# Two terms of a split product as one 512-column matmul in the feed-forward output and down projections

## The chip, the cores and the metric

The kernel runs on one core of a Trainium2 chip. The metric is device time in microseconds, the median of several executions. TensorE multiplies; its weight loads have a row of their own in the profile (PEld), because a load can lie under the matmul before it. VectorE (DVE), ScalarE (ACT) and GpSimd (POOL) do elementwise work, SyncE (SP) issues the transfers of the weights. PSUM, where matmuls write, is here one tensor `bank` of eight banks, each 512 fp32 wide on each of the 128 partitions.

## The reference, cut to what matters

The program is two layers of one transformer block and two layers of another on 256 tokens of width 1024. The places of this change are the second products of the feed-forward parts:

```
def _swiglu(x, w_in, w_out):
    gate, up = jnp.split(x @ w_in, 2, axis=-1)
    return (jax.nn.silu(gate) * up) @ w_out
...
h = h + 0.5 * g1[:, None, :] * _swiglu(hn, ffn1_w_in[l], ffn1_w_out[l])     # D_FF = 2816
...
h = h + 0.5 * g3[:, None, :] * _swiglu(hn, ffn2_w_in[l], ffn2_w_out[l])
...
return x + jnp.square(jax.nn.relu(h @ w_up)) @ w_down                       # 4 * 1024 wide inside
```

The output must be as exact as fp32 products.

## The kernel before

**Split products.** A matmul on fp32 data is slow, one on rounded data (fp32r) is fast but inexact. So each factor is held as two rounded parts, the high part and the rest, and a product is three terms: high weight times high input, high weight times low input, low weight times high input. `terms` (lines 714 to 720) issues them one after another into the same 256 columns of a PSUM bank. Each matmul loads its 128x128 block of weights first, so the high weights are loaded twice.

**Where the weights come from.** SyncE fills a ring of four slots (`ring`) by DMA, 256 columns of the weights at a time ("a chunk"). ScalarE rounds a half chunk into `w_hi` (line 1210), GpSimd subtracts it from the ring and leaves the rest in `w_lo` (line 685), and TensorE waits for that (`half_ready`). `w_hi` and `w_lo` hold two chunks, so there are four half chunks in flight, and ScalarE may overwrite a half when TensorE has used it.

**Order of the work.** All engines run hand-ordered lists. For each of the two layers of part one: `ffn("f1")`, the mixing stage (projection "z", attention, projection "o"), `ffn("f2")`. For each of the two layers of part two: the projection "z2" with attention between its pieces, "y" and "wo", "up" and "dn". An `ffn` is an input product of 22 chunks of 8 tiles (line 719 with `hn` and `hn_lo`), and the output product `out_product` with 4 groups of 256 output columns. In a group the inner 2816 are 22 tiles of 128, brought in four chunks of 6, 6, 5 and 5 tiles; in "dn" there are 32 tiles in four chunks of 8. A group has two output tiles `c` of 128 rows (the weight's columns) by 256 tokens; each has a bank of its own, of which the first 256 columns are used. In each half chunk `out_product` does all tiles of `c` = 0, then all of `c` = 1.

**Inputs of the product.** `gated` (feed-forward) and `up2` (down) hold for each tile the high part (index 0) and the low part (index 1), 256 columns each, side by side.

**After a group.** VectorE adds the bank to the residual `h`: line 1709 (`stt`: bank times gate plus `h`) in `ffn`, line 2070 (`tt`) after "dn", once for `c` = 0, once for `c` = 1. ScalarE squares the new `h` (line 1238), VectorE sums the squares (`add_squares`, line 1626), TensorE sums over the partitions (lines 815 and 818), ScalarE makes the root (lines 1244 and 1246), and the scaled `h` feeds the next stage's first product (lines 750, 751 and 754). That chain stands at the end of each `ffn` and each "dn"; nothing else can feed TensorE in it.

**Small fp32 products.** Some matmuls take unrounded fp32: the attention scores (line 934), group sums (line 1012, 512 columns), the projections "o" and "wo" (line 805), the sums of ada weights (line 842).

Of the kernel before, what the change touches and what calls it, by code (L numbers as in the profile page):

```python
# [20 lines left out]
ALU = mybir.AluOpType  # L21
# [5 lines left out]
S = 256  # L27
# [284 lines left out]
def out_bank(g, c):  # L312

    return 2 - 2 * (g % 2) + c
# [73 lines left out]
def build(nc, dram, out, at, old):  # L389

    plan = Plan()
    with ExitStack() as ctx:
# [307 lines left out]
        def _(pe):  # L700
# [60 lines left out]
                        last.then_inc(weights_used, eng.step(f"used {phase} {i}" if half else  # L761
                                                             f"half used {phase} {i}", weights_used))

            def out_product(phase, chunks, x, outs, done, free, last_x):

                total = sum(k_tiles(phase, i)[1] for i in chunks)
                for i in chunks:
                    q = split_slot(phase, i)  # L770
                    if last_x and i == chunks[-1]:
                        pe.wait_ge(parts_done, eng.at(last_x))
                    for half, (k0, n) in enumerate(halves(phase, i)):
                        half_ready(phase, i, half)
                        for c in range(2):
                            if i == chunks[0] and half == 0:
                                for by, mark in free[c:c + 1]:
                                    pe.wait_ge(by, eng.at(mark))
                            ws = slice(c * P, (c + 1) * P)
                            for k in range(n):  # L780
                                kx, kw = k_tiles(phase, i)[0] + k0 + k, half * 4 + k
                                last = terms(outs[c], w_hi[:, q, kw, ws], w_lo[:, q, kw, ws], x[:, kx, 0], x[:, kx, 1],
                                             False, kx == 0, kx == total - 1)
                            if c == 1:
                                last.then_inc(weights_used, eng.step(f"used {phase} {i}" if half else
                                                                     f"half used {phase} {i}", weights_used))
                            elif half and i == chunks[-1]:
                                last.then_inc(tensor_done, eng.step(done))
# [105 lines left out]
            def ffn(s, layer, following):  # L894
                for p in range(PAIRS):
                    for r in range(2):
                        b = bank[:, 2 * (p % 2) + r].rearrange("p (c s) -> p c s", c=2)
                        free = ((silu_done, f"{s} hi {p - 2}") if r else (parts_done, f"{s} gated {p - 2}"),)
                        product(s + "in", (2 * p + r,), (b[:, 0], b[:, 1]), first=s if p == r == 0 else None,
                                free=free if p >= 2 else ())  # L900
                    if (s, p) in (("f1", 9), ("f2", 8)):
                        ada_fold(layer, 0 if s == "f1" else 2)
                for g in range(4):
                    out_product(s + "out", tuple(range(4 * g, 4 * g + 4)), gated,
                                (bank[:, out_bank(g, 0), 0:S], bank[:, out_bank(g, 1), 0:S]), f"{s} out {g}",
                                ((vector_done, f"h {following} {2 * g - 4}"), (vector_done, f"h {following} {2 * g - 3}"))
                                if g >= 2 else ((parts_done, f"{s} gated {PAIRS - 2}"),) if g == 0 else (),
                                f"{s} gated {PAIRS - 1}" if g == 0 else None)
# [174 lines left out]
            for layer in eng.layers("two"):  # L1083
# [62 lines left out]
                        norm_sum("up")  # L1146
                for g in range(4):
                    out_product("dn", tuple(range(4 * g, 4 * g + 4)), up2,
                                (bank[:, 2 * (g % 2), 0:S], bank[:, 2 * (g % 2) + 1, 0:S]), f"dn out {g}",
                                ((vector_done, f"h {AFTER_DN[layer]} {2 * g - 4}"), (vector_done, f"h {AFTER_DN[layer]} {2 * g - 3}"))  # L1150
                                if g >= 2 else ((parts_done, "up split 13"),) if g == 0 else (),
                                "up split 15" if g == 0 else None)
# [418 lines left out]
        def _(dve):  # L1571
# [105 lines left out]
            def ffn(s, gate_at, layer, following):  # L1677
                for p in range(PAIRS):
                    j = p % 2
                    if (s, p) == ("f2", 9):  # L1680
                        modulation(layer, 64, 72, (layer, 17))
                    of = ada_chunk(s + "in", p, layer)
                    if of:
                        ada_sum(*of)
                    dve.wait_ge(silu_done, eng.at(f"{s} silu {p}"))
                    dve.wait_ge(weights_used, eng.at(f"used {s}in {2 * p + 1}"))
                    tt(bank[:, 2 * j], act_tmp[:, j], bank[:, 2 * j + 1], ALU.mult) \  # L1687
                        .then_inc(vector_done, eng.step(f"{s} mult {p}"))
                    dve.wait_ge(silu_done, eng.at(f"{s} hi {p}"))
                    tt(gated[:, 2 * p:2 * p + 2, 1, :], bank[:, 2 * j].rearrange("p (c s) -> p c s", c=2),  # L1690
                       gated[:, 2 * p:2 * p + 2, 0, :], ALU.subtract).then_inc(parts_done, eng.step(f"{s} gated {p}", parts_done))
                if s == "f1":
                    modulation(layer, 16, 48, (layer, 11))
                ts(der[:, 24:32], mod[:, gate_at:gate_at + 8], 0.5, None, ALU.mult) \
                    .then_inc(vector_done, eng.step())
                dve.wait_ge(vector_done, eng.at())
                for g in range(4):
                    of = ada_chunk(s + "out", g, layer)
                    if of:
                        ada_sum(*of)  # L1700
                    if g:
                        add_squares(following, g - 1)
                    for c in range(2):
                        k = 2 * g + c
                        if c == 0:
                            dve.wait_ge(tensor_done, eng.at(f"{s} out {g}"))
                        else:
                            dve.wait_ge(weights_used, eng.at(f"used {s}out {4 * g + 3}"))
                        stt(h[:, k], bank[:, out_bank(g, c), 0:S], col(der, 24 + k), h[:, k], ALU.mult, ALU.add) \
                            .then_inc(vector_done, eng.step(f"h {following} {k}"))  # L1710

            def maxima(hd, tile, maps=(0, 1, 2)):
                st = stat[:, hd.u % 4]
# [262 lines left out]
            for layer in eng.layers("two"):  # L1976
# [84 lines left out]
                for g in range(4):  # L2061
                    if g:
                        add_squares(AFTER_DN[layer], g - 1)
                    for c in range(2):
# [2 lines left out]
                            dve.wait_ge(tensor_done, eng.at(f"dn out {g}"))  # L2067
                        else:
                            dve.wait_ge(weights_used, eng.at(f"used dn {4 * g + 3}"))
                        tt(h[:, k], bank[:, 2 * (g % 2) + c, 0:S], h[:, k], ALU.add) \  # L2070
                            .then_inc(vector_done, eng.step(f"h {AFTER_DN[layer]} {k}"))
                        if layer + 1 == L:
                            dve.wait_ge(vector_done, eng.at())
                            ts(result[:, k], h[:, k], col(norm2, 32 + k), None, ALU.mult) \
# [24 lines left out]
```

## Time and profile before

| what | value |
|---|---|
| median of 3 executions | 2004.17 us (2003.87, 2004.17, 2008.47) |
| span of the profiled execution | 2008.3 us |
| execution nearest to it by time, with what lies around the span | 2008.47 us |
| TensorE busy | 1929.0 us, 96% of the span, 15200 matmuls and as many loads |
| GpSimd busy | 1321.1 us, 66% |
| ScalarE busy | 940.1 us, 47% |
| VectorE busy | 837.2 us, 42% |
| chain that ended last | TensorE 84%, line 719 alone 68% |

Busy time of TensorE says only that some matmul was in its pipeline: matmuls overlap, and a 256-column one is recorded with some 280 ns while the next begins less than 120 ns later. The distance from one start to the next is what costs time; it is read from starts in the timeline, or from a merged piece of the chain of waits divided by its count. Times in the rows are in microseconds from the start of the span, mean durations in ns.

### The profile page before, as it was taken

The page shows a single profiled execution, that of the slowest core. Times are in us where ns is not written, and L with a number is a line of the kernel's source. Part 1 is how long each engine was busy: PE and PEld are TensorE (multiplying, and loading weights), DVE is VectorE, ACT ScalarE, POOL GpSimd, SP SyncE. Part 2 cuts the span into 40 slices and gives each one's busy share as a digit, 9 for nine tenths or more (in the row PEclk, how much of TensorE's full clock was granted, in tenths as well). Part 3 has the DMA queues.
Part 4 walks back from the last instruction along what each step waited for, and adds up shares of the span by engine and source line. Part 5 has one row for each costly group of instructions (what it writes and reads, how often), then busy time and mean ns, then how long its engine had stood idle before and what let it go on. Part 6 is the DMA issues. An engine that isn't in the chain of part 4 may idle for free.

```text
span 2008.3 us, 36107 instructions
## 1 busy us (share of the span) xinstructions
PE 1929.0 (96%) x15200; PEld 1859.7 (93%) x15200; DVE 837.2 (42%) x1753; ACT 940.1 (47%) x1467; POOL 1321.1 (66%) x612
## 2 busy tenths in 40 slices
PE   6999997999999999889999999999999999999999
PEld 3999995899999998779999999989999999999999
DVE  3774676372148467735112532233311622233322
ACT  2544454344454445445444445525544445535543
POOL 0878770388878887316887965506896964506896
PEclk8999999999999999899999999999999999999999
DMA  9999650695589886227555643336564643336652
GB/s 325 360 344 312 198 189 22 221 363 170 177 293 367 303 267 187 86 76 262 192 164 168 213 158 112 121 131 189 191 210 148 210 148 113 122 128 189 203 199 98
DMA packets 357074, 398.01 MB, mean 198 GB/s; under 512 B 9016, under 2 KB 319024, under 8 KB 356912
## 3 DMA queue, kind: packets, MB, share of 16 engines
q1 hardware_dynamic: 356752, 395.50, 59.5%
q8 instruction: 120, 1.97, 0.4%
q14 instruction: 42, 0.34, 0.0%
q10 hardware_dynamic: 160, 0.20, 0.0%
HBM read 394.62 MB, written 1.05 MB: 197 GB/s over the span
## 4 chain that ended last, share of the span: by engine, by line
PE 84%; DVE 4%; SPq 3%; ACT 3%; POOL 2%; DMA 1%; issue 1%; ACTq 0%; DVEq 0%
PE bank L719 68%; PE bank L805 6%; PE bank L1131 3%; POOL w_lo L685 2%; PE bank L968 1%; PE bank L934 1%; SPq L580 1%; DVE arena L1730 1%; SPq L547 1%; ACT w_hi L1210 1%; DVE bank L1659 1%; ACT arena L1346 1%; PE bank L750 1%; DVE arena L1774 1%; SPq L590 1%
## 5 line engine op out<-in xcount | busy, mean ns | idle before, releaser
L685 POOL TENSOR_TENSOR w_lo<-ring,w_hi 128x1024 fp32r<-128x1024 f32 (+2 forms) x608 | 1320.9, 2196 | 672.3 <-ACT w_hi L1210 671.7
L719 PE MATMUL bank<-hn,w_hi 128*128 128x256 f32 x2752 | 773.7, 281 | 8.6 <-POOL w_lo L685 8.1
L1210 ACT ACTIVATE w_hi<-ring 128x1024 fp32r<-128x1024 f32 (+2 forms) x608 | 578.3, 976 | 413.1 <-PE bank L719 368.0
L719 PE MATMUL bank<-hn,w_lo 128*128 128x256 f32 x2752 | 766.4, 278 | 0.0
L719 PE MATMUL bank<-hn_lo,w_hi 128*128 128x256 f32 x2752 | 766.3, 278 | 0.0
L719 PEld LDWEIGHTS bank<-hn,w_hi 128*128 128x128 f32 x2752 | 517.9, 188 | 12.4 <-POOL w_lo L685 7.3
L719 PEld LDWEIGHTS bank<-hn_lo,w_hi 128*128 128x128 f32 x2752 | 520.2, 189 | 1.0 <-issue 0.5
L719 PEld LDWEIGHTS bank<-hn,w_lo 128*128 128x128 f32 x2752 | 517.7, 188 | 0.0
L719 PE MATMUL bank<-gated,w_hi 128*128 128x256 f32 x1408 | 248.9, 281 | 0.0
L719 PEld LDWEIGHTS bank<-gated,w_hi 128*128 128x128 f32 x1408 | 216.8, 190 | 0.0
L719 PE MATMUL bank<-gated,w_lo 128*128 128x256 f32 x704 | 198.0, 281 | 0.0
L719 PE MATMUL bank<-up,w_hi 128*128 128x256 f32 x1024 | 174.2, 276 | 0.0
L1587 DVE SCALAR_TENSOR_TENSOR bank<-arena,cond,bank 128x512 f32<-128x512 f32 x204 | 154.2, 756 | 7.3
L719 PEld LDWEIGHTS bank<-up,w_hi 128*128 128x128 f32 x1024 | 154.0, 188 | 0.0
L719 PE MATMUL bank<-up,w_lo 128*128 128x256 f32 x512 | 141.4, 276 | 0.0
L719 PEld LDWEIGHTS bank<-gated,w_lo 128*128 128x128 f32 x704 | 132.2, 188 | 0.0
L805 PE MATMUL bank<-arena,ring 128*128 128x256 f32 x512 | 113.3, 383 | 3.2 <-ACT arena L1464 3.2
L805 PEld LDWEIGHTS bank<-arena,ring 128*128 128x128 f32 x512 | 98.3, 193 | 17.0 <-ACT arena L1464 3.6
L1687 DVE TENSOR_TENSOR bank<-arena,bank 128x512 f32<-128x512 f32 x44 | 30.6, 695 | 198.0 <-PE bank L719 198.0
L1298 ACT ACTIVATE arena<-bank 128x512 f32<-128x512 f32 x44 | 26.3, 598 | 165.0 <-PE bank L719 164.4
L1346 ACT ACTIVATE arena<-arena,stat 128x128 f32<-128x128 f32 x120 | 53.2, 445 | 101.3 <-DVE stat L1744 43.5
L719 PEld LDWEIGHTS bank<-up,w_lo 128*128 128x128 f32 x512 | 96.1, 188 | 0.0
(214 smaller groups left out, 2206.0 us busy)
## 6 DMA issues: line engine op xcount, KB each, us to landing
ring<-in_ffn_w_in SPq DMA_DIRECT2D x88, 1024.0 KB, 7.2
ring<-in_w_in SPq DMA_DIRECT2D x72, 1024.0 KB, 5.1
arena<-in_ada_w SPq DMA_DIRECT2D x35, 2048.0 KB, 10.5
ring<-in_w_up SPq DMA_DIRECT2D x32, 1024.0 KB, 5.5
ring<-in_w_down SPq DMA_DIRECT2D x32, 1024.0 KB, 5.0
ring<-in_ffn_w_out SPq DMA_DIRECT2D x32, 768.0 KB, 5.5
ring<-in_ffn_w_out SPq DMA_DIRECT2D x32, 640.0 KB, 4.1
ring<-in_w_in SPq DMA_DIRECT2D x16, 512.0 KB, 3.6
```

What stands on the lines that cost most here:

```text
L547: sp.dma_start(dst, src).then_inc(rows_in, 16)
L580: sp.dma_start(ring[:, s, k:k + n, :], src).then_inc(weights_in[s], 16)
L590: sp.dma_start(dst, src).then_inc(params_in, 16)
L685: pool.tensor_tensor(w_lo[:, q, ks], ring[:, r, k0:k0 + n], w_hi[:, q, ks], ALU.subtract) \
L719: last = mm(out, a, b, start=start and i == 0, stop=stop and i == 2)
L805: last = mm(outs[c], ring[:, s, k, c * P:(c + 1) * P], x[:, k, :], start=not begun and j == 0, stop=ends and j == len(ks) - 1)
L1131: last = mm(b[:, c], ring[:, s, k0 + k, c * P:(c + 1) * P], o2[:, k0 + k, :], start=(k == 0), stop=(k == nk - 1))
L1210: f(w_hi[:, q, half * 4:half * 4 + n], ring[:, r, k0:k0 + n], ACT.Copy).then_inc(weights_rounded, 1)
L1298: f(act_tmp[:, j], bank[:, 2 * j], ACT.Silu).then_inc(silu_done, eng.step(f"{s} silu {p}", silu_done))
L1346: f(t, t, ACT.Exp, bias=st[:, b + j:b + j + 1], scale=scale, accum_out=st[:, 10 + 2 * m + j:11 + 2 * m + j]) \
L1587: stt(part, src[:, k], col(cond, k), part, ALU.mult, ALU.add).then_inc(vector_done, eng.step())
L1687: tt(bank[:, 2 * j], act_tmp[:, j], bank[:, 2 * j + 1], ALU.mult) \
```

## The change

In `out_product` the three terms of a tile become two matmuls: the high weights times both parts of the input side by side, 512 columns into the whole bank (high times high in columns 0 to 255, high times low in 256 to 511), and the low weights times the high part, 256 columns, added into the first half. The sum of the two halves is formed by VectorE: it adds each half to `h` with an operation of its own, the second waiting for the first.

```
-            def out_product(phase, chunks, x, outs, done, free, last_x):
+            def out_product(phase, chunks, x, banks, done, free, last_x):
...
+                            both, first = bank[:, banks[c]], bank[:, banks[c], 0:S]
+                            kx, kw = k_tiles(phase, i)[0] + k0, half * 4
                             for k in range(n):
-                                kx, kw = k_tiles(phase, i)[0] + k0 + k, half * 4 + k
-                                last = terms(outs[c], w_hi[:, q, kw, ws], w_lo[:, q, kw, ws], x[:, kx, 0], x[:, kx, 1],
-                                             False, kx == 0, kx == total - 1)
+                                mm(both, w_hi[:, q, kw + k, ws], x[:, kx + k].rearrange("p a s -> p (a s)"),
+                                   start=kx + k == 0, stop=False, skip_group_check=True)
+                                last = mm(first, w_lo[:, q, kw + k, ws], x[:, kx + k, 0], start=False,
+                                          stop=kx + k == total - 1, skip_group_check=True)
...
-                        stt(h[:, k], bank[:, out_bank(g, c), 0:S], col(der, 24 + k), h[:, k], ALU.mult, ALU.add) \
-                            .then_inc(vector_done, eng.step(f"h {following} {k}"))
+                        for a in range(2):
+                            stt(h[:, k], bank[:, out_bank(g, c), a * S:(a + 1) * S], col(der, 24 + k), h[:, k],
+                                ALU.mult, ALU.add).then_inc(vector_done, eng.step(f"h {following} {k}" if a else None))
+                            if a == 0:
+                                dve.wait_ge(vector_done, eng.at())
...
-                        tt(h[:, k], bank[:, 2 * (g % 2) + c, 0:S], h[:, k], ALU.add) \
-                            .then_inc(vector_done, eng.step(f"h {AFTER_DN[layer]} {k}"))
+                        for a in range(2):
+                            tt(h[:, k], bank[:, 2 * (g % 2) + c, a * S:(a + 1) * S], h[:, k], ALU.add) \
+                                .then_inc(vector_done, eng.step(f"h {AFTER_DN[layer]} {k}" if a else None))
+                            if a == 0:
+                                dve.wait_ge(vector_done, eng.at())
```

TensorE, the beginning of the first output product, before (x2 is two rows that read alike):

```order
L719 MATMUL bank<-hn,w_lo 128x256
L719 MATMUL bank<-gated,w_hi 128x256 x2
L719 MATMUL bank<-gated,w_lo 128x256
L719 MATMUL bank<-gated,w_hi 128x256 x2
L719 MATMUL bank<-gated,w_lo 128x256
```

The same place now:

```order
L719 MATMUL bank<-hn,w_lo 128x256
L783 MATMUL bank<-gated,w_hi 128x512
L785 MATMUL bank<-gated,w_lo 128x256
L783 MATMUL bank<-gated,w_hi 128x512
L785 MATMUL bank<-gated,w_lo 128x256
```

Two 256-column rows on the same weights have become one of 512 columns; the low weights' row stands where it stood, and nothing else on TensorE moved.

VectorE, the end of the first `ffn` (the last group's residual, then small work for the next stage, then the scaled `h`), before:

```order
L1626 TENSOR_TENSOR square_sum<-square,bank 128x256
L1709 SCALAR_TENSOR_TENSOR h<-bank,der,h 128x256 x2
L1674 SCALAR_TENSOR_TENSOR der<-mod,arena 128x8
```

The same place now:

```order
L1629 TENSOR_TENSOR square_sum<-square,bank 128x256
L1713 SCALAR_TENSOR_TENSOR h<-bank,der,h 128x256 x4
L1677 SCALAR_TENSOR_TENSOR der<-mod,arena 128x8
```

Four residual operations stand where there were two, in each of the 16 groups of the four `ffn`, and likewise in the 8 groups of "dn".

## Rows read from the trace of the kernel before

**Rows 1.** The page, chain that ended last, shares of the span by line

```profile
PE bank L719 68%; PE bank L805 6%; PE bank L1131 3%; POOL w_lo L685 2%; PE bank L968 1%; PE bank L934 1%; SPq L580 1%; DVE arena L1730 1%; SPq L547 1%; ACT w_hi L1210 1%; DVE bank L1659 1%; ACT arena L1346 1%; PE bank L750 1%; DVE arena L1774 1%; SPq L590 1%
```

**Rows 2.** The chain in order of time: start, us, engine and line, count

```profile
486.94 84.89 PE bank L719 x720
583.27 103.36 PE bank L719 x912
687.45 73.58 PE bank L719 x624
1378.66 168.67 PE bank L719 x1488
```

**Rows 3.** Instruction groups by shape: count, busy us, mean ns, idle before

```profile
L719 PE MATMUL bank<-gated,w_lo 128*128 128x256 f32 x704 | 198.0, 281 | 0.0
L719 PE MATMUL bank<-up,w_lo 128*128 128x256 f32 x512 | 141.4, 276 | 0.0
```

**Rows 4.** Timeline, first product after a norm: start, us, engine, instruction

```profile
577.61 0.41 PE L750 MATMUL bank<-hn,w_hi 128*128 128x256 f32 x1
577.82 0.41 PE L751 MATMUL bank<-hn,w_lo 128*128 128x256 f32 x1
```

**Rows 5.** Stretches: busy us (count) of each engine, granted clock, DMA share, GB/s

```profile
577.50:580.30 2.80, 2.80 (x15) 2.80 (x15) 2.68 (x7) 2.26 (x4) 0.31 (x1) 0.50 0.81 257
1548.50:1551.10 2.60, 0.48 (x2) 0.11 (x2) 0.99 (x3) 1.63 (x5) 1.26 (x1) 1.00 0.02 6
```

**Rows 6.** Timeline of the weight loads of eight 32-column matmuls

```profile
686.36 0.97 PEld L842 LDWEIGHTS bank<-arena,const 128*128 128x128 f32 x8
```

**Rows 7.** Timeline inside an output product, a load and its neighbours

```profile
219.74 0.40 PE L719 MATMUL bank<-gated,w_hi 128*128 128x256 f32 x2
219.75 0.19 PEld L719 LDWEIGHTS bank<-gated,w_hi 128*128 128x128 f32 x1
```

**Rows 8.** Weight loads around a long fp32 matmul, 256 and 512 columns

```profile
1173.02 0.19 PEld L719 LDWEIGHTS bank<-w_hi,hn 128*128 128x128 f32 x1
1173.23 0.19 PEld L719 LDWEIGHTS bank<-w_hi,hn_lo 128*128 128x128 f32 x1
1173.35 0.19 PEld L719 LDWEIGHTS bank<-w_lo,hn 128*128 128x128 f32 x1
...
266.75 0.19 PEld L719 LDWEIGHTS bank<-w_hi,hn 128*128 128x128 f32 x1 [0.24 <-issue]
267.17 0.19 PEld L719 LDWEIGHTS bank<-w_hi,hn_lo 128*128 128x128 f32 x1 [0.24 <-issue]
267.29 0.19 PEld L719 LDWEIGHTS bank<-w_lo,hn 128*128 128x128 f32 x1
```

**Rows 9.** The chain in order of time, projection "o", fp32 matmuls of 256 columns

```profile
354.51 24.19 PE bank L805 x112
```

**Rows 10.** GpSimd's groups from 1020 to 1080 us, then from 1464 to 1544

```profile
L685 POOL TENSOR_TENSOR w_lo<-ring,w_hi 128x768 fp32r<-128x768 f32 x22 | 40.1, 1852 | 8.1 <-ACT w_hi L1210 8.1
L685 POOL TENSOR_TENSOR w_lo<-ring,w_hi 128x512 fp32r<-128x512 f32 x6 | 7.8, 1295 | 0.0
...
L685 POOL TENSOR_TENSOR w_lo<-ring,w_hi 128x1024 fp32r<-128x1024 f32 x30 | 71.6, 2398 | 7.1 <-ACT w_hi L1210 7.1
```

**Rows 11.** Timeline of VectorE, residual of an `ffn` tail and of a "dn" tail

```profile
571.16 0.48 DVE L1709 SCALAR_TENSOR_TENSOR h<-bank,der,h 128x256 f32<-128x256 f32 x1 [12.70 <-PE bank L719]
571.87 0.48 DVE L1709 SCALAR_TENSOR_TENSOR h<-bank,der,h 128x256 f32<-128x256 f32 x1 [0.23 <-PE bank L719]
...
1546.00 0.43 DVE L2070 TENSOR_TENSOR h<-bank,h 128x256 f32<-128x256 f32 x1 [18.05 <-PE bank L719]
...
1547.36 0.42 DVE L2070 TENSOR_TENSOR h<-bank,h 128x256 f32<-128x256 f32 x1 [0.93 <-PE bank L719]
```

**Rows 12.** Timeline of VectorE, two dependent sums in a row

```profile
229.42 0.43 DVE L1626 TENSOR_TENSOR bank<-square,bank 128x256 f32<-128x256 f32 x1
229.88 0.42 DVE L1626 TENSOR_TENSOR square_sum<-square,bank 128x256 f32<-128x256 f32 x1
```

More of the change, by code:

```diff
@@ L904, in ffn @@
                     out_product(s + "out", tuple(range(4 * g, 4 * g + 4)), gated,
-                                (bank[:, out_bank(g, 0), 0:S], bank[:, out_bank(g, 1), 0:S]), f"{s} out {g}",
+                                (out_bank(g, 0), out_bank(g, 1)), f"{s} out {g}",
                                 ((vector_done, f"h {following} {2 * g - 4}"), (vector_done, f"h {following} {2 * g - 3}"))
@@ L1148, in _ @@
                     out_product("dn", tuple(range(4 * g, 4 * g + 4)), up2,
-                                (bank[:, 2 * (g % 2), 0:S], bank[:, 2 * (g % 2) + 1, 0:S]), f"dn out {g}",
+                                (2 * (g % 2), 2 * (g % 2) + 1), f"dn out {g}",
                                 ((vector_done, f"h {AFTER_DN[layer]} {2 * g - 4}"), (vector_done, f"h {AFTER_DN[layer]} {2 * g - 3}"))
```

## The prediction, on record before the changed kernel ran

> **What bounds the kernel now.** I read the chain of waits first. Line 719, the split product, is 68% of the span [rows 1], and its long pieces are unbroken runs of TensorE in which nobody else ends a wait [rows 2]. The output and down products lie inside such runs: the groups on `gated` and `up` have no idle time before them [rows 3]. So a nanosecond less per tile there is a nanosecond less of span, as long as TensorE stays the last to arrive.
>
> Then the distance between matmuls. Dividing the pieces of [rows 2] by their counts gives two values: 84.89 / 720 = 117.9 ns and 73.58 / 624 = 117.9 ns, but 103.36 / 912 = 113.3 ns and 168.67 / 1488 = 113.4 ns. All are 256-column matmuls at the full granted clock. The first two hold the output products of `ffn` (the product on `gated` runs at 117.9), the last holds "up" and "dn" of a layer (113.4).
>
> What is a matmul made of? At the half clock (0.50, 1.2 GHz [rows 5]) the same shape starts every 577.82 - 577.61 = 213 ns [rows 4]; this is 256 columns at 1.2 GHz, one column a cycle with nothing on top. At 2.4 GHz the columns therefore need 106.7 ns, and 7 to 11 ns of each distance are something else. It is the weight load: eight matmuls of only 32 columns still load every (0.97 - 0.19) / 7 = 111 ns [rows 6], and a load starts only when the matmul before it has started (219.74 and 219.75 [rows 7]). So the chain is load, matmul start, load, and the columns hide just under the load. Where the columns are long, the load is hidden instead: fp32 matmuls of 256 columns, which take twice the cycles, start every 24.19 / 112 = 216 ns [rows 9], 213.3 of columns and 2.7 of handover.
>
> **The change part by part.**
>
> *One of three loads goes.* Per tile: before, three distances; now a 512-column stream (213.3 ns of columns) under which the load of the low weights is hidden, then a 256-column one under which the next high load is not. The trace has just this pair, with an fp32 matmul of 256 columns in the role of the long one: loads start with the matmuls at 1173.02, 1173.23 and 1173.35 [rows 8], so 0.33 us from the start of the long one to the end of the short one; 0.21 and 0.12. Behind the 512-column fp32 one it is again 267.29 - 267.17 = 0.12 [rows 8]. I take 216 + 117.5 = 333 ns a tile; a short distance does not come out at 113 right behind a hidden load in these rows.
>
> *In `ffn`*: 704 tiles (one w_lo matmul each [rows 3]) at 3 x 117.9 = 353.7 ns, now 333: 20.7 x 704 = 14.6 us saved. *In "dn"*: 512 tiles [rows 3] at 3 x 113.4 = 340.2, now 333: 7.2 x 512 = 3.7 us. Together 18.3 us.
>
> *Bounds of this term.* No row shows an fp32r matmul of 512 columns. The best it can be is the columns alone, 320 ns a tile: 33.7 x 704 + 20.2 x 512 = 34.1 us. The worst that a row suggests is the fp32 one of 512 columns, 267.17 - 266.75 = 0.42 us [rows 8], so 0.54 a tile: (540 - 353.7) x 704 + (540 - 340.2) x 512 = 233 us lost. I take the value by the half-clock rows, where fp32r takes a column a cycle.
>
> *The supply of low weights has to keep up.* GpSimd takes 1.852 us for three tiles, 1.295 for two, 2.398 for four [rows 10]. A group of 22 tiles is six pieces of three and two of two: 6 x 1.852 + 2 x 1.295 = 13.7 us, TensorE's part of it now 44 x 0.333 = 14.7 us (15.6 before). In "dn" it is 2.40 against 8 x 0.333 = 2.66. So GpSimd goes from 88% to 93%, in "dn" to 90%, and stays below. Its waits of 8.1 and 7.1 us are for `w_hi` [rows 10], which ScalarE may write only when TensorE has used the half before: they follow TensorE's pace and should shrink with it. I cost this at nothing; if that cover is gone, each tenth of a microsecond per piece costs 128 x 0.1 = 13 us in `ffn`.
>
> *Twice as many residual operations.* 48 more on VectorE. In the middle groups nobody waits: it stood idle 12.70 us before the last group's [rows 11], and the banks are wanted again two groups on. At the six ends they are on the path, since the next norm needs `h`. In `ffn`: `c` = 0 ends its matmuls before 571.16, `c` = 1 is ready 0.71 later [rows 11] (two tiles). Now two dependent operations for `c` = 0 take 0.48 + 0.03 + 0.48 (the gap from [rows 12]: 229.88 - 229.42 - 0.43), so `c` = 1 starts at +1.02 instead of +0.71, and ends at +2.01 where it was +1.19: 0.82 us late. In "dn", `c` = 1 is ready 1.36 us after `c` = 0 [rows 11]; two operations (0.89) fit in, and only one more (0.43 + 0.03) is added behind: 0.46. Sum 4 x 0.82 + 2 x 0.46 = 4.2 us lost. Nothing can go the other way here.
>
> *The gaps at the norms get longer.* Behind such gaps TensorE is sometimes found at 1.2 GHz (577.5 to 580.3 [rows 5]) and sometimes not (1548.5 to 1551.1 has 1.00 with TensorE almost idle [rows 5]). A piece of some 3 us at the half clock, in a stretch where VectorE sets the pace anyway, I put at 0 to 1.7 us; for three more of them 0 to 5 us. I take 0.
>
> **Sum.** 18.3 - 4.2 = 14.1 us off. The profiled execution has a span of 2008.3 and matches the 2008.47 of the runs: it becomes 1994.4. Two of three runs lie 4.3 us lower. That is the size of one input product with its neighbours at 113.4 instead of 117.9 (4.5 ns x about 950 matmuls), so I think runs differ by the distance into which a stage falls. I forecast against the median: 2004.17 - 14.1 = 1990.
>
> **The rivals.**
>
> *The short matmul also hides its load* (or the distance falls to 113 behind it). Then 216 + 106.7 = 322.7 ns a tile: 31.0 x 704 + 17.5 x 512 = 30.8, less 4.2: 26.6 off, 1977.5. For it: the 216 of [rows 9] shows a hidden load costs only 2.7. Against it: [rows 6], a load needs 111 and begins with the matmul of 106.7, and the 0.12 of [rows 8]. Halfway, with 113.4 for the short one (329.4), it is 17.1 + 5.5 - 4.2 = 18.4 off, 1986. The Trainium skill, page "TensorE: Matmul & The Clock Gate", section "Back-to-back issue gap", gives N / 2.4 + 2.5 ns between matmuls, 216 for 512 columns and 109 for 256, 325 for the pair; by it alone the time would be an estimated 1980. The 216 of [rows 9] agrees, the 113 and 118 of [rows 2] do not agree with 109. The same page, section "LDWEIGHTS (loading the stationary operand)", puts a load of 128 columns at 128 / 1.2 = 107 ns, where [rows 6] has 111.
>
> *A 512-column fp32r matmul is dearer than its columns* (slower than before). Place: each of the 1216 tiles. The change breaks even where 704 x (353.7 - x) + 512 x (340.2 - x) = 4.2 us, x = 344.6 ns a tile, so from 227 ns for the 512-column matmul on, 14 more than its columns. At the fp32 price of [rows 8] the time is 2004 + 233 + 4 = 2241. For it: no row of this shape. Against it: [rows 4].
>
> *The supply sets the pace.* If GpSimd's waits for `w_hi` stay what they are, nothing is won in the products, the tails cost 4.2: 2008. TensorE would show waits for line 685 in these stretches, which now has none. Against it: two whole chunks of cover.
>
> *Other stages fall into the longer distance* or the clock falls at more norms: + 4.5 us each time, 1995 to 2003.
>
> **How the numbers follow.** Forecast (a tile at 330 to 336 ns) 0.52, its own range 1986 to 1997; short matmul quicker 0.20; other stages or the clock against it 0.13; supply 0.08; dear 512 columns 0.07. About 0.3% (6 us) is what a measurement of this kernel tells from none, so faster means under 1998.2: 0.52 + 0.20 and two thirds of 0.13, 0.81. Same: the rest of 0.13 and most of the supply case, 0.12. Slower 0.07. The range 1978 to 2001 leaves out part of the quickest case, supply and dear columns.
>
> **What would show it.** Lines 783 and 785 start a pair every 0.33 us in all six products, with a load on every matmul; the loads hidden under line 783 stand 0.21 apart from the next. Chain pieces of the output products: 528 matmuls of `ffn` at 117.9 (62 us) become 352 in 58.6 us; "dn" goes from 87 to 85.3. VectorE's residual before a norm ends 0.8 later against the last matmul. I am wrong if the pair is not within 326 to 338, if line 685 ends TensorE's waits there, or if a stage without any edit changes by more than 5 us.

## The result, and the profile after

| | median us | runs | ratio to before, 95% interval |
|---|---|---|---|
| before | 2004.99 (2003.87 to 2008.47) | 4 | |
| changed | 2016.74 (2015.43 to 2022.01) | 4 | 1.0053 [1.0031, 1.0076] |

The forecast was 1990 us, with 2001 as its upper end. The change made the kernel 0.5% slower. Beside the experiments with a ratio below, the kernel before was run again, with medians of 2006.1 to 2008.3 us; each ratio is against those runs. The profiled execution of the changed kernel has a span of 2013.6 us (2015.43 with what lies around it) at a mean granted clock of 0.986.

The page of the changed kernel, chain and groups (count, then busy us and mean ns), where the split product is now divided over lines 719, 783 and 785:

```profile
PE bank L719 46%; PE bank L783 14%; PE bank L785 7%; PE bank L808 6%; PE bank L1134 3%; POOL w_lo L685 2%; PE bank L971 1%; PE bank L937 1%; SPq L580 1%; DVE arena L1736 1%; SPq L547 1%; PE bank L750 1%; ACT w_hi L1213 1%; ACT arena L1349 1%; PE bank L754 1%
...
L783 PE MATMUL bank<-gated,w_hi 128*128 128x512 f32 x704 | 248.9, 397 | 0.0
L785 PE MATMUL bank<-gated,w_lo 128*128 128x256 f32 x704 | 197.8, 281 | 0.0
```

Against [rows 1 and 3], the three lines together still have 46 + 14 + 7 = 67% where line 719 had 68%. The products are as long as before. Their busy times overlap, since the next matmul starts before the recorded 397 or 281 ns are over, so they don't give the distance. That comes from the timeline of TensorE: the last of the input product and the beginning of an output product, then its end (start us, us, engine, line):

```profile
508.41 0.28 PE L719 MATMUL bank<-hn,w_lo 128*128 128x256 f32 x1
508.53 0.39 PE L783 MATMUL bank<-gated,w_hi 128*128 128x512 f32 x1
508.76 0.28 PE L785 MATMUL bank<-gated,w_lo 128*128 128x256 f32 x1
...
509.22 0.40 PE L783 MATMUL bank<-gated,w_hi 128*128 128x512 f32 x1
509.46 0.28 PE L785 MATMUL bank<-gated,w_lo 128*128 128x256 f32 x1
...
570.35 0.40 PE L783 MATMUL bank<-gated,w_hi 128*128 128x512 f32 x1
570.58 0.28 PE L785 MATMUL bank<-gated,w_lo 128*128 128x256 f32 x1
```

From 508.53 to 570.58 there are 175 pairs and one 512-column distance. In the rows the next matmul starts 0.24 us after a 512-column one (235 ns in 698 of 704 cases) and 0.12 after a 256-column one (118). A pair takes 353.3 ns, where three matmuls took 353.5. So 528 instructions in 62.07 us became 352 in 62.05. The weight loads do lie as predicted, one beginning with each matmul (PEld timeline of the changed kernel):

```profile
508.53 0.19 PEld L785 LDWEIGHTS bank<-gated,w_lo 128*128 128x128 f32 x1
508.76 0.19 PEld L783 LDWEIGHTS bank<-gated,w_hi 128*128 128x128 f32 x1
```

The down product comes out of a stretch with matmuls every 113.4 ns (TensorE timeline, same columns):

```profile
1457.58 0.28 PE L719 MATMUL bank<-hn,w_lo 128*128 128x256 f32 x1
1457.69 0.39 PE L783 MATMUL bank<-up,w_hi 128*128 128x512 f32 x1
1457.91 0.28 PE L785 MATMUL bank<-up,w_lo 128*128 128x256 f32 x1
1458.03 0.40 PE L783 MATMUL bank<-up,w_hi 128*128 128x512 f32 x1
1458.27 0.28 PE L785 MATMUL bank<-up,w_lo 128*128 128x256 f32 x1
```

Its first 512-column matmul takes 0.22 us, every later one 0.24. A tile that took 340 ns takes 353.3.

The tail of an output product: VectorE's residual, then TensorE's first matmul behind the norm (two timelines of the changed kernel, one engine each):

```profile
570.20 1.91 DVE L1713 SCALAR_TENSOR_TENSOR h<-bank,der,h 128x256 f32<-128x256 f32 x4 [12.65 <-PE bank L785]
```

```profile
575.50 0.35 PE L750 MATMUL bank<-hn,w_hi 128*128 128x256 f32 x1 [2.19 <-ACT hn L1273]
```

Before, the second residual ended at 571.87 + 0.48 = 572.35 [rows 11], 0.80 us after the start of the last matmul (571.55). Now it is 570.20 + 1.91 - 570.58 = 1.53: 0.73 later. The four operations take 1.91 us, not the 2.01 of the prediction: the third, on the other bank, is recorded as starting 0.08 us before the second ends. GpSimd in the same kind of stretch (1028 to 1091 us), by shape:

```profile
L685 POOL TENSOR_TENSOR w_lo<-ring,w_hi 128x768 fp32r<-128x768 f32 x22 | 40.2, 1850 | 7.4 <-ACT w_hi L1213 7.4
L685 POOL TENSOR_TENSOR w_lo<-ring,w_hi 128x512 fp32r<-128x512 f32 x11 | 14.2, 1288 | 1.9 <-ACT w_hi L1213 1.8
```

It still idles for `w_hi`, as in [rows 10], and inside the product the trace has no wait of TensorE for another engine.

All stages, as us from the start of the first to the start of the last matmul of a stretch, each worked out from the two traces:

| stretch | before | changed |
|---|---|---|
| output product, four times | 62.07 | 62.05 to 62.07 |
| down product, twice | 86.93 | 90.33 |
| output product to the next product | 4.19, 4.19, 4.19, 4.12 | 4.91, 4.91, 4.92, 4.84 |
| down product to next / to the last matmul | 4.06 / 3.17 | 4.53 / 3.63 |
| long part of input product 2, by layer | 103.25, 103.25 | 103.29, 99.43 |
| attention to the norm sum behind projection "o", first time | 68.57 | 66.20 |

The first four rows give -0.04 + 6.80 + 2.89 + 0.93 = 10.6 us, against 0.0053 x 2005 = 10.6 by the ratio. The last two rows have no edit in them. The input product took either some 99.4 or 103.3 us in the two layers of the changed kernel alone, where the code is the same, and these two rows (6.2 us together) account for most of why the two profiled spans lie only 5.3 us apart.

### The profile page after: what moved, and what is told of

Same layout as the page of the kernel before. It is cut to its first block, busy times and chain, and to the rows that moved or that the text cites. A ratio compares the mean times of both kernels' runs of the same rounds, so it can differ in the third digit from the quotient of the medians.

```text
span 2013.6 us, 33723 instructions
## 1 busy us (share of the span) xinstructions
PE 1929.8 (96%) x13984; PEld 1806.1 (90%) x13984; DVE 857.2 (43%) x1801; ACT 941.8 (47%) x1467; POOL 1321.8 (66%) x612
## 4 chain that ended last, share of the span: by engine, by line
PE 84%; DVE 4%; SPq 3%; ACT 3%; POOL 2%; DMA 1%; issue 1%; ACTq 0%; DVEq 0%
PE bank L719 46%; PE bank L783 14%; PE bank L785 7%; PE bank L808 6%; PE bank L1134 3%; POOL w_lo L685 2%; PE bank L971 1%; PE bank L937 1%; SPq L580 1%; DVE arena L1736 1%; SPq L547 1%; PE bank L750 1%; ACT w_hi L1213 1%; ACT arena L1349 1%; PE bank L754 1%
## 5 line engine op out<-in xcount | busy, mean ns | idle before, releaser
L783 PE MATMUL bank<-gated,w_hi 128*128 128x512 f32 x704 | 248.9, 397 | 0.0
L783 PE MATMUL bank<-up,w_hi 128*128 128x512 f32 x512 | 181.0, 397 | 0.0
L783 PEld LDWEIGHTS bank<-gated,w_hi 128*128 128x128 f32 x704 | 132.4, 188 | 32.5
L783 PEld LDWEIGHTS bank<-up,w_hi 128*128 128x128 f32 x512 | 96.3, 188 | 23.7
```

Source lines behind the costliest of these rows:

```text
L783: mm(both, w_hi[:, q, kw + k, ws], x[:, kx + k].rearrange("p a s -> p (a s)"), start=kx + k == 0, stop=False, skip_group_check=True)
```

## Experiments

Two theories at first. **Stream theory**: a rounded (fp32r) matmul's own stream costs more than a column a cycle at the full clock, so joining two into one removes no time. **Second-load theory**: the stream is cheap, and something in the pair (the load of other weights, two halves of a bank, the alternation) costs the time. Later a third question came in: what sets 113.3 or 117.9 ns.

A summary of the whole kernels, from each profiled execution (us, first to last start):

| kernel | output product | down product | tails | ratio, interval |
|---|---|---|---|---|
| ffn_only | 62.05 to 62.07 | 86.93 | 4.92; 4.06, 3.17 | 1.0012 [0.9995, 1.003] |
| three_halves | 62.07 | 86.93 | 4.92; 4.53, 3.62 | 1.0031 [1.0014, 1.0048] |
| one_residual | 62.05 to 62.07 | 90.33 | 4.19; 4.07, 3.17 | 1.0036 [1.0022, 1.0051] |
| grouped | 61.07 | 88.63 | 4.92; 4.52, 3.62 | 1.0022 [1.0008, 1.0036] |
| spare_fold | 59.73 | 86.93 | 4.19; 4.06, 3.17 | 0.9952 [0.9934, 0.997] |
| changed_fold | 62.06 | 90.33 | 4.92; 4.53, 3.62 | 1.0044 [1.0026, 1.0062] |

**m1_streams: streams of equal matmuls.** It computes nothing of the reference; each stream changes the weights with every matmul.

```
for i in range(96):
    a, k = go(i, 96, 1, wr, xr, 512)      # likewise 256, 320, 384; 32 or 64 weight columns; fp32; bf16
    last = mm(*a, **k)
```

> A small kernel of matmul streams alone (it computes nothing of the reference). Read from the trace: the distance from start to start in each stream, at the full clock, with 128-row weights unless said. Theory S, a rounded (fp32r) stream simply moves at 0.443 to 0.459 ns a column, whatever is loaded meanwhile: 256 columns 113 to 118 ns, 320 142 to 147, 384 170 to 176, 512 227 to 235, and the same 227 to 235 and 113 to 118 when the weights have only 32 columns. Theory C, the columns move at 0.417 ns and the load of the next weights steals time from the stream that it lies under: with weights of 32 columns a 512-column matmul falls to 214 to 220 ns and a 256-column one to 107 to 112, and 64-column weights lie between. Theory L, that of the prediction (the load bounds a 256-column matmul and is free under a longer one): 320 columns 136, 384 columns 163, 512 columns 216.

The chain of waits in order of time (start, us, line, count). Lines: 68 and 89 fp32r 256 columns, 71 fp32r 512, 77 fp32r 384, 80 fp32r 512 with 32-column weights, 86 fp32r 256 with 64-column weights, 92 fp32 256, 101 bf16 512, 104 bf16 256:

```profile
18.14 24.93 PE bank L68 x192
43.07 21.79 PE bank L71 x96
...
76.37 16.65 PE bank L77 x96
93.02 22.24 PE bank L80 x96
...
126.15 10.88 PE bank L86 x96
137.03 11.52 PE bank L89 x96
148.55 20.72 PE bank L92 x96
...
221.99 20.72 PE bank L101 x96
242.71 10.48 PE bank L104 x96
```

Divided by the counts: fp32r 512 columns 227.0 ns (226.7 start to start in the steady part), bf16 512 columns 215.8, fp32 256 columns 215.8; fp32r 256 columns 120.0 with full weights (line 89; line 68 begins with 15 distances of 213 ns, as at the half clock, which raises its mean) and 113.3 with 64 or 32 columns of weights, bf16 109.2. The recorded weight loads, by line:

```profile
L92 PEld LDWEIGHTS bank<-x,w 128*128 128x128 f32 x96 | 18.2, 190 | 2.4
L71 PEld LDWEIGHTS bank<-xr,wr 128*128 128x128 f32 x96 | 18.0, 188 | 3.7
```

Each fp32 matmul of the code is two rows (48 make the x96 of line 92), and a row takes two cycles a column: 429.2 ns for 512 columns (line 98), 215.8 for 256. So an fp32 row of 256 columns and an fp32r matmul of 512 need the same 213.3 ns for their columns and have loads of the same length, and yet one takes 215.8 and the other 227.0. With a load of only 32 columns the long fp32r stream gets no shorter (231.7). So the load is not what fills the time above the columns of a long stream. Of a 256-column one the load has a share here: 120.0 falls to 113.3 with narrow weights, and the other 6.7 ns above the columns stay.

In cycles of 2.4 GHz, 113.3 ns is 272 = 256 x 17/16, and 226.7 is 544 = 512 x 17/16. The widths between don't follow that factor: 384 columns took 173.4 and 320 took 146.7 (170.0 and 141.7 by it), each some 13.3 above its bare columns, as are 120.0 and 226.7. Of the three theories S has all these values but the 120.0; C and L have the long streams wrong. The Trainium skill, page "TensorE: Matmul & The Clock Gate", section "Back-to-back issue gap", gives N / 2.4 + 2.5 ns; the bf16 rows agree (216 and 109), the fp32r rows (227 and 113 to 120) do not. The same section's sustained 131 ns for 512 columns is not seen in any stream here.

**e3_three_halves: the changed kernel's outputs and residuals, but each 512-column matmul as two of 256.**

```diff
+    second = bank[:, banks[c], S:2 * S]
-    mm(both, w_hi[:, q, kw + k, ws], x[:, kx + k].rearrange("p a s -> p (a s)"), start=kx + k == 0, ...)
+    mm(first, w_hi[:, q, kw + k, ws], x[:, kx + k, 0], start=kx + k == 0, ...)
+    mm(second, w_hi[:, q, kw + k, ws], x[:, kx + k, 1], start=False, ...)
```

> Three matmuls of 256 columns as in the kernel before, but the middle term goes to the second half of the bank, and VectorE adds both halves as in the changed kernel. If the whole loss in the products comes from the 512-column form: products as before (117.9 ns a matmul in the feed-forward, 113.4 in the down product), only the six tails longer, 4 x 0.86 + 2 x 0.46: 2009.3 us, 1.002 times before. If instead writing to two halves of a bank is what costs: the down product goes to 118 ns a matmul too and the time to 2016.

TensorE's timeline at the start of an output product:

```profile
504.62 0.28 PE L784 MATMUL bank<-gated,w_hi 128*128 128x256 f32 x1
504.74 0.28 PE L786 MATMUL bank<-gated,w_hi 128*128 128x256 f32 x1
504.86 0.28 PE L788 MATMUL bank<-gated,w_lo 128*128 128x256 f32 x1
```

A tile is 0.35 us, as with the pair. Three separate matmuls are as fast as the pair in `ffn`, and 3.4 us faster in each down product; both halves of the bank are in use here too, so they are no cause. Only the tails remain (3.8 us, 0.19%; the ratio is 1.0031, with 1.0014 in its interval).

**e4_one_residual: the changed kernel, VectorE adds only the first half of each bank.** Its result leaves out the product of high weights and low input parts.

```diff
-    for a in range(2):
-        stt(h[:, k], bank[:, out_bank(g, c), a * S:(a + 1) * S], ...)
+    stt(h[:, k], bank[:, out_bank(g, c), 0:S], col(der, 24 + k), h[:, k], ALU.mult, ALU.add)
```

> The 512-column form as in the changed kernel, but VectorE adds only the first half (the high weight times low input term is left out of the result). If the second residual operation costs 4.3 us at the six tails: 2016.7 - 4.3 = 2012.4 us. If it costs nothing on the path and all of the loss is in the products: 2016.7.

All tails return to 4.19, 4.12, 4.07 and 3.17 us, the products keep 62.05 and 90.33. So the tails cost 3.8 us and the pairs 6.8, each without the other.

**e1_ffn_only: the pair in `ffn`, three matmuls and one residual in "dn".**

```diff
+    if phase != "dn":
         (the pair)
+    else:
+        last = terms(first, w_hi[...], w_lo[...], x[:, kx + k, 0], x[:, kx + k, 1], False, ...)
```

> The change in the feed-forward output products alone; the down products are as before. If a 512-column matmul costs exactly two of 256 at 117.6 ns: these products take the same time as before, the four tails cost 3.4 us, and the down products are back at 113.4: 2008.4 us, 1.0017 times before. If the new form disturbs the stages behind it (clock or distance), more than 2011.

The down products are back at 86.93. What is left is the four `ffn` tails: 2.9 us, 0.14%, inside the interval, which also holds no change at all; it is the rows that show this cost.

**m2_pairs and m3_tiles: mixtures** (nothing of the reference is computed).

In the code the numbers behind # are the lines that the rows name; `hi` and `lo` are different weight blocks.

```
for i in range(64):
    mm(bank[:, 1], hi(i), xs(i, 0, 512), ...)        # 75
    mm(bank[:, 1, 0:256], lo(i), xs(i, 0, 256), ...) # 76; 108: hi(i) again; 111/112: bf16; m3 123/124: 64-column weights
```

> A second small kernel of matmul streams alone (it computes nothing of the reference). Measured so far: rounded matmuls of one size in a row take 120.0 ns (256 columns), 146.7 (320), 173.3 (384), 226.7 (512), each its columns at 2.4 GHz and 13.3 ns more, and in the changed kernel the pair takes 235 + 118 = 353. Theory P, a price per matmul (13.3 ns, 6.7 in a luckier phase): the pair of 512 and 256 takes 340 to 347 ns, the triple of 256 takes 340 to 360, 384 + 384 takes 347, 448 columns 200, 288 columns 133, and four of 512 followed by four of 256 the same 340 to 347 a tile. Theory X, the alternation of two lengths is what costs: the pair takes 353 here too, and 340 to 347 when four of a length stand together. Theory K, the other engines' traffic in the kernel costs it: the pair takes 340 to 347 here in every order, and grouping changes nothing in the kernel. If the load of different weights matters, the pair on one weight block differs from the pair on two.

> A third small kernel of streams alone (it computes nothing of the reference). The pair of 512 and 256 rounded columns took 353.3 ns there and in the changed kernel, 325 in bf16. If the loads of different weights under the streams cost it, the pair with weights of 32 columns falls below 335 ns and the one with 64 between; if the rounded stream has its own price, they stay at 340 to 353. If the place of the tiles matters, the pair and the triple on separate tensors differ from the 353.3 and 360.0 of one tensor; a single tile for weights and input gives 113.3 and 226.7. Eight small fp32 matmuls ahead should leave the triple at 118 to 120, two long ones at 113 to 116, if the phase is set by what runs ahead.

TensorE's timeline of m2_pairs: the pair, the pair on one set of weights, the pair in bf16:

```profile
60.08 0.40 PE L75 MATMUL bank<-xr,wr 128*128 128x512 f32 x1
60.32 0.28 PE L76 MATMUL bank<-xr,wr 128*128 128x256 f32 x1
60.44 0.40 PE L75 MATMUL bank<-xr,wr 128*128 128x512 f32 x1
...
228.58 0.39 PE L107 MATMUL bank<-xr,wr 128*128 128x512 f32 x1
228.81 0.28 PE L108 MATMUL bank<-xr,wr 128*128 128x256 f32 x1
228.92 0.39 PE L107 MATMUL bank<-xr,wr 128*128 128x512 f32 x1
...
251.10 0.38 PE L111 MATMUL bank<-xb,wb 128*128 128x512 bf16 x1
251.32 0.27 PE L112 MATMUL bank<-xb,wb 128*128 128x256 bf16 x1
251.43 0.38 PE L111 MATMUL bank<-xb,wb 128*128 128x512 bf16 x1
```

And of m3_tiles, the pair with weights of 64 columns:

```profile
248.50 0.39 PE L123 MATMUL bank<-xr,wr 128*64 128x512 f32 x1
248.73 0.27 PE L124 MATMUL bank<-xr,wl 128*64 128x256 f32 x1
```

Over the 64 pairs of each: 353.3 ns, 346.7 on the same weights, 325.0 in bf16, 340.0 with 64-column weights (343.3 with 32). 340.0 ns is 768 columns x 17/16 / 2.4 GHz, the three 113.3 that "dn" already had. Full weights add 13.3 to that, and half of it goes when both matmuls of a pair use one block. Both theories have a share: the stream theory the larger one (340 against the 320 of bare columns), the other 13.3. A pair in two banks took 353.4 and one with the two weight blocks in tensors of their own 353.1, so neither is the cause, and no other engine works beside these streams. Four long ones followed by four short ones took 350.6 a tile, and two matmuls of 384 columns 346.7; so of the theories on record X had the 353 of the pair, but not the 350.6, P had the 346.7 and 360.0, but not the pair, and K, that other engines cause it, is out.

Three matmuls took 360.0 (3 x 120.0) in every mixture, also behind short or long fp32 matmuls, so these programs don't reproduce the 113.3 of "dn" for full weights. Against 360.0 the pair saves 6.7 ns a tile; in the kernel, where three matmuls take 353.5 or 340, it saves nothing.

**e5_grouped: the changed kernel with the high products of a half chunk first, then the low ones.**

```diff
     for k in range(n):
         mm(both, w_hi[...], ...)
+    for k in range(n):
         last = mm(first, w_lo[...], ...)
```

> As the changed kernel, but in each half chunk all 512-column matmuls of a column tile come first, then all 256-column ones (runs of 2 to 4). Theory X: a tile goes from 353.3 to 340 to 347 ns, so the four output products take 60 to 61 us (62.05 in the changed kernel) and the two down products 87 to 88.8 (90.33); 4 to 16 us faster than the changed kernel, at or slightly below the kernel before. Theories P and K: 62.05 and 90.33 stay, 2016.

TensorE's timeline in the down product (x4 are four matmuls in a row):

```profile
1480.05 1.09 PE L783 MATMUL bank<-up,w_hi 128*128 128x512 f32 x4
1480.98 0.62 PE L786 MATMUL bank<-up,w_lo 128*128 128x256 f32 x4
```

Four long ones take 0.93 us (1480.98 - 1480.05), and by the whole product (88.63 us for 512 matmuls) a tile is 347 ns. Less alternation takes 1.0 us off an output product and 1.7 off a down product, not more. Even so a tile stays above the 340 of "dn" before.

**e6_spare: which work ahead sets the distance.** Kernel before, with spare fp32 matmuls into a bank that is free there: after each fold of the modulation (1 x 256, 2 x 256, 1 x 128, 1 x 512 columns in turn), and eight of 32 columns ahead of the down product of layer 0 alone.

```diff
+    def spare(cols, times):
+        for _ in range(times):
+            mm(bank[:, 4, 0:cols], ones, tab("cos", cols), start=True, stop=True, ...)
     ada_fold(layer, 0 if s == "f1" else 2)
+    spare(*SPARE[s, layer])
 ...
+    if layer == 0:
+        spare(32, 8)
```

> The kernel before with spare fp32 matmuls (constants into an unused bank) behind the ada fold of each feed-forward part: 1 of 256 columns (f1 of layer 0), 2 of 256 (f2 of layer 0), 1 of 128 (f1 of layer 1), 1 of 512 (f2 of layer 1); and eight of 32 columns ahead of the down product of layer 0, none in layer 1. State theory: 113.4 or 117.9 ns a 256-column matmul is a phase that the stream keeps and that is set by what runs just ahead of it, not by its tiles. Then the first down product takes 90.3 us (117.6 ns) and the second 86.93 (113.2), and one or more of the four output products drops from 62.07 to 59.8 us. Tile theory: the feed-forward's addresses cost 117.9 and the down product's 113.4; then all six stay where they are, 62.07 and 86.93 us, whatever stands ahead.

The chain in order of time (start, us, count): the rest of an input product with its output product in layer 0; then "up" and "dn" of layer 0, and of layer 1:

```profile
481.01 81.62 PE bank L720 x720
...
1363.46 81.62 PE bank L720 x720
1446.78 90.55 PE bank L720 x768
...
1824.64 168.66 PE bank L720 x1488
```

The 84.89 us of [rows 2] became 81.62 for the same 720 matmuls: 113.4 instead of 117.9. "dn" of layer 0 went the other way, 90.55 / 768 = 117.9, while layer 1 without the short matmuls kept 168.66. All four output products took 59.73 us, whichever spare one stood ahead. So the distance is a state of the stream: at these places short fp32 matmuls (four in a fold, which are eight rows, or the eight spare ones ahead of "dn") bring the long distance, a single fp32 matmul of 128 columns or more behind them the short one, and the stream keeps it until a wait or another kind of matmul interrupts it. It is no rule for every place: in the mixing stage of the kernel before, the matmuls behind the 512-column fp32 ones at 266, 273 and 285 us start every 118 ns, and in m3_tiles two long fp32 matmuls left the stream at 120.0. This kernel was executed once, 2002.46 us beside 2001.36 of the kernel before; single executions of one kernel lie over 10 us apart, so the whole time says nothing here.

**e7_spare_fold: kernel before with one spare 128-column fp32 matmul after each fold, and nothing else.**

```diff
     ada_fold(layer, 0 if s == "f1" else 2)
+    spare(128, 1)
```

> The kernel before with one spare fp32 matmul of 128 columns behind each of the four ada folds, nothing else. State theory, and the measurement with four kinds of spare matmuls: each output product takes 59.7 instead of 62.07 us and the rest of the input product behind the fold 0.8 us less, the spare 0.1 to 0.2 more: 4 x 2.5 = 10 us off, 0.995 times before, with the down products at 86.93. If the gain seen in the trace is taken back elsewhere (the next norm, the supply of low weights): 1.000.

Its chain of waits, for the same pieces:

```profile
480.17 81.61 PE bank L719 x720
...
994.10 81.61 PE bank L719 x720
```

1997.96 us median (9 runs) beside 2008.28: 0.9952 [0.9934, 0.997]. This beats both kernels. By stages it is 4 x 2.34 = 9.4 us in the output products and some 1.6 in what is left of the input products (2.5 less 4 x 0.22 for the spare ones).

**e8_spare_more: eight more spare ones inside the input products** (after pairs 2 and 5 of each).

> The same, and a spare matmul also after the second and the fifth pair of each input product, so eight more. If a spare matmul brings any stream to 113.4 ns: the input product of f2, which takes 99.4 or 103.25 us from one execution to the next, is always near 99.6 and the first f1 shortens by about 1 us: some 2 us less in the mean than with the four alone, and less scatter between executions. If a spare matmul can also throw a stream out of 113.4, the input products get longer and this is the slower of the two.

0.9951 [0.9933, 0.9968], no more than e7_spare_fold. The stretches behind the added ones start every 113.7 ns, but most did already. One that had the long distance, at the beginning of `f1` in layer 1, went over to the short one behind the first added matmul. In layer 0 the rest of that input product took 46.97 us for 384 matmuls, against 43.50 in layer 1: three waits for GpSimd (2.3 us) stand in it, and one of its four pieces between them ran at the long distance, the others at the short one. So a wait can change the distance, and need not.

**e9_changed_fold: the changed kernel with the same four spare matmuls.**

> This is the changed kernel with one spare fp32 matmul of 128 columns after each of the four ada folds, the edit that brought the output products of the kernel before from 62.07 to 59.73 us each. Theory (a 512-column matmul followed by a 256-column one on other weights takes 353.3 ns whatever the products before it ran at, because the rounded stream needs 17/16 of a cycle a column and the exchange of weights adds 13 ns to a pair): the four output products stay at 62.05 us and the down products at 90.33, only the remainder of the input product behind each fold goes from 22.58 to 21.74 us, so 4 x 0.84 less 4 x 0.1 for the spare ones, about 3 us under the changed kernel's time: 2012 to 2015 us, 0.6 to 0.8% above the kernel with the same spare matmuls and three 256-column products (1998). Rival (the pair is also quicker when the products before it start at 113.3 ns: 340 to 347 ns a tile): the output products take 59.7 to 60.9 us, and the time is 2004 to 2010.

TensorE's timeline into an output product that now comes from the short distance:

```profile
507.18 0.28 PE L719 MATMUL bank<-hn_lo,w_hi 128*128 128x256 f32 x1
507.29 0.28 PE L719 MATMUL bank<-hn,w_lo 128*128 128x256 f32 x1
507.41 0.39 PE L783 MATMUL bank<-gated,w_hi 128*128 128x512 f32 x1
507.63 0.28 PE L785 MATMUL bank<-gated,w_lo 128*128 128x256 f32 x1
507.75 0.40 PE L783 MATMUL bank<-gated,w_hi 128*128 128x512 f32 x1
507.99 0.28 PE L785 MATMUL bank<-gated,w_lo 128*128 128x256 f32 x1
```

The first 512-column matmul takes 0.22 us, the rest 0.24, as in the down product. The output product stays at 62.06 us, where three matmuls with the same spare ones take 59.73. The median of 2016.45 is a little above the 2012 to 2015 expected, its interval [1.0026, 1.0062] reaches down to them; the output products came out as the theory had them. Of the "4 x 0.84" only two stretches are that long (21.74 us for 192 matmuls); the other two, with 96, give 0.4 each. The rival is refuted: in all six products the pair takes 353.3 ns, out of either distance.

## Why the prediction was wrong

**The step that failed** is "at 2.4 GHz the columns therefore need 106.7 ns, and 7 to 11 ns of each distance are something else. It is the weight load". The half-clock distance was carried to the full clock. But the shortest distances seen of an fp32r stream at the full clock are 113.3 and 226.7 ns for 256 and 512 columns: 6.7 and 13.3 above the bare columns, and loads of 32 or 64 columns take nothing more off. So of the 7 to 11 ns that the prediction gave to an exposed load, 6.7 belong to the stream, and a joined stream has them in full; the rest, 4.6 ns in `ffn`, is the distance that e6_spare and e7_spare_fold took away with one spare matmul and the loads unchanged. Only in the small programs did a full load cost a 256-column matmul anything (120.0 against 113.3). That the 111 ns of [rows 6] lie so near 113.3 made the load look like the bound; no run shows that it is one.

**The 512-column matmul**, taken as 216 ns, is 226.7 in a stream of its own and 235 next to one on other weights. The 216 came from [rows 9], an fp32 matmul; m1_streams has fp32 at that value and fp32r 11 ns above it. It is the term of the sum that was wrong by 19 ns, in each of 1216 tiles. **The short one** was right as a number: 117.5 predicted, 118 measured. Its reason, an exposed load, isn't shown, so that was luck in part. A tile: 353.3, not 333. In `ffn` 14.6 us of saving became 0; in "dn" 3.7 us became a loss of 6.8, since the pair takes 353.3 also where three matmuls took 340.

**The rival that came true** was "a 512-column fp32r matmul is dearer than its columns". Its break-even of 227 ns is the value of the pure stream; within the pair it was 8 above. It had 0.07, because [rows 4] was read as speaking against it. Its only price, fp32's 0.42 us, was far off, and no smaller one was worked out.

**Right**: the tails (0.82 forecast and 0.73 measured in `ffn`, 0.46 and 0.47 in "dn"; together 4.2 and 3.8 us), shown alone by e4_one_residual. The 0.1 us too much in `ffn` is the third operation, which was taken to start behind the second. GpSimd's supply was not put to the test, as TensorE didn't become faster. The clock behind the longer norm gaps cost nothing: what follows them took the same before and now, 110.62 us for the input product of `f1` in layer 1, 25.8 for each first piece of "z", 73.4 for each first piece of "z2".

**Half right** was "runs differ by the distance into which a stage falls". The unedited input product of `f2` does come out at 99.3 to 99.6 or at 103.3 us from trace to trace and from layer to layer. But the output and down products took 62.07 and 86.93 us in every trace in which they and what stands ahead of them were unedited, and e6_spare set the distance both ways.

**Open**: why the fp32r stream takes more than its columns at the full clock (213 ns at the half clock [rows 4] is bare columns), why full weights add 13.3 ns a pair, and what in the matmuls ahead sets the distance. The programs here show all three and explain none.

## What to carry to other kernels

The fp32r distance at the half clock was bare columns and at the full clock it was not; so before streams are joined, measure one long stream of that very type at the clock that counts, once with full and once with narrow weights, to part column time from load time, and then the very mixture that will run: the pair took 353.3 ns where its two streams alone take 226.7 and 120.0. In this kernel the joined stream saved nothing in `ffn` and lost 13 ns a tile in "dn", while the doubled epilogue (the residual operations behind each product) cost 0.5 to 0.7 us at every product that a norm waits for. Where identical products run at two distances, look at the few matmuls ahead of them.

## What was not expected of the hardware

- The 113.3 and 117.9 are states that last for hundreds of matmuls. Ahead of the output products the four fp32 matmuls of 8 to 32 columns bring the longer one, one of 128 columns behind them (0.3 us in the chain) the shorter; it is worth 0.5% of this kernel.
- A 512 + 256 pair of fp32r takes 353.3 ns out of either state, 346.7 on one set of weights, 340.0 with weights of 64 columns.
